# Second feed-forward matmul of a transformer block by seven half-size products over two hidden blocks

## The reference

```python
D_MODEL = 1024; SEQ = 1024; D_FF = 4 * D_MODEL; PLE_DIM = 256
x = x + jnp.concatenate([y_lru, y_att], axis=-1) @ w_out[i]
h = rmsnorm(x, g_ffn[i])
x = x + jnp.square(jax.nn.relu(h @ w_ff1[i])) @ w_ff2[i]
gate = jax.nn.sigmoid(rmsnorm(x, g_ple[i]) @ w_ple_gate[i])
x = x + gate * (p[i] @ w_ple_proj[i])
return rmsnorm(x, g_final)
```

## Time and profile before

| | |
|---|---|
| median of 3 runs | 1074.56 us (1074.12 to 1074.68) |
| profiled execution, first to last instruction | 1072.1 us (its whole time isn't given apart; the median of the runs is 2.5 us above this span) |
| TensorE busy | 1063.0 us, 99% |
| VectorE, ScalarE, GpSimd busy | 680.3, 468.1, 416.6 us |
| passes of the second matmul | 1536, 199.8 + 199.2 + 199.2 us of overlapping durations |
| loads of hidden weights in the loop | 60 of 512 KB, landing 3.8 us after issue |

### The profile page before, as it was taken

The page is one execution under the profiler, slowest core; times in us unless marked ns, Lnnn a source line. Parts: engine busy times, 40 slices in busy tenths (PEclk is TensorE's granted clock), DMA queues, the critical chain, the costliest instruction groups (busy, mean ns, idle before and its releaser), DMA issues.

```text
span 1072.1 us, 13889 instructions
## 1 busy us (share of the span) xinstructions
PE 1063.0 (99%) x4960; PEld 869.5 (81%) x4960; DVE 680.3 (63%) x932; ACT 468.1 (44%) x806; POOL 416.6 (39%) x282
## 2 busy tenths in 40 slices
PE   9999999999999999999999999999999999999997
PEld 7877787777887888888888888888888888888897
DVE  7988787888799643644544544544544544697648
ACT  7467836555683332332332322322322422566334
POOL 0000061334136626516426425435435445295221
PEclk9999999999999999999999999999999999999999
DMA  8111110111011121121111111112112112420004
GB/s 335 40 40 40 40 58 32 40 41 40 0 40 40 40 79 39 39 78 39 39 70 48 39 49 69 39 39 78 39 39 78 39 39 76 159 79 1 1 2 158
DMA packets 20179, 61.06 MB, mean 57 GB/s; under 512 B 2096, under 2 KB 4144, under 8 KB 20144
## 3 DMA queue, kind: packets, MB, share of 16 engines
q1 hardware_dynamic: 19312, 59.56, 15.3%
q10 hardware_dynamic: 832, 1.05, 0.3%
HBM read 56.40 MB, written 4.19 MB: 57 GB/s over the span
## 4 chain that ended last, share of the span: by engine, by line
PE 89%; DVE 6%; ACT 3%; issue 1%; DMA 1%; SPq 0%; POOL 0%; DVEq 0%; ACTq 0%; POOLq 0%
PE bank L611 29%; PE bank L612 28%; PE bank L613 28%; PE bank L726 1%; PE bank L697 1%; ACT raw L1191 1%; DMA stage<-in_w_in 1%; DVE xT L1849 1%; DVE t_lo L1798 1%; PE bank L741 0%; PE bank L756 0%; DVE raw L1792 0%; ACT h_hi L1183 0%; DVE r_ffn L1433 0%; DVE r_mix L1433 0%
## 5 line engine op out<-in xcount | busy, mean ns | idle before, releaser
L611 PE MATMUL bank<-h_hi,w_hi 128*128 128x512 f32 (+1 forms) x722 | 278.5, 386 | 0.6 <-DVE w_lo L1428 0.5
L612 PE MATMUL bank<-h_lo,w_hi 128*128 128x512 f32 (+1 forms) x722 | 274.6, 380 | 0.0
L613 PE MATMUL bank<-h_hi,w_lo 128*128 128x512 f32 (+1 forms) x722 | 274.5, 380 | 0.0
L1849 DVE TENSOR_TENSOR xT<-bank,xT 128x512 f32<-128x512 f32 x256 | 172.3, 688 | 109.8 <-PE bank L613 109.8
L611 PE MATMUL bank<-u_hi,w_hi 128*128 128x512 f32 x512 | 199.8, 390 | 0.2
L613 PE MATMUL bank<-u_hi,w_lo 128*128 128x512 f32 x512 | 199.2, 389 | 0.0
L612 PE MATMUL bank<-u_lo,w_hi 128*128 128x512 f32 x512 | 199.2, 389 | 0.0
L611 PEld LDWEIGHTS bank<-h_hi,w_hi 128*128 128x128 f32 x722 | 135.7, 188 | 35.1 <-issue 6.6
L613 PEld LDWEIGHTS bank<-h_hi,w_lo 128*128 128x128 f32 x722 | 135.8, 188 | 26.1
L612 PEld LDWEIGHTS bank<-h_lo,w_hi 128*128 128x128 f32 x722 | 135.8, 188 | 25.4 <-issue 0.5
L557 POOL TENSOR_TENSOR w_lo<-w_raw,w_hi 128x1024 fp32r<-128x1024 f32 x30 | 73.9, 2485 | 125.6 <-ACT w_hi L1283 117.8
(11 more groups left out here) (238 smaller groups left out, 1727.9 us busy)
## 6 DMA issues: line engine op xcount, KB each, us to landing
w_raw<-in_w_ff SPq DMA_DIRECT2D x60, 512.0 KB, 3.8
stage<-in_w_in SPq DMA_DIRECT2D x13, 512.0 KB, 6.6
stage<-in_w_out SPq DMA_DIRECT2D x8, 512.0 KB, 4.5
stage<-in_w_ple_gate SPq DMA_DIRECT2D x8, 512.0 KB, 3.2
xT<-in_x SPq DMA_DIRECT2D x6, 512.0 KB, 10.9
stage<-in_w_ff SPq DMA_DIRECT2D x4, 512.0 KB, 3.2
out_x<-xT SPq DMA_DIRECT2D x4, 512.0 KB, 3.1
out_x<-xT SPq DMA_DIRECT2D x6, 256.0 KB, 2.2
```

The source lines that it names most:

```text
L611: pe.matmul(o, whi, hh, start=first, stop=False, skip_group_check=onto)
L612: pe.matmul(o, whi, hl, start=False, stop=False, skip_group_check=onto)
L613: return pe.matmul(o, wlo, hh, start=False, stop=last, skip_group_check=onto)
L1849: dve.tensor_tensor(dst, bank[4 + q % 4][:, :], dst, ALU.add).then_inc(y_added, 1)
```

## The change

Blocks 2 to 15 are taken in seven pairs `g`, 1 to 7. In each pair the first matmul is computed as before, 7 products for block s = 0 and 7 for s = 1 (`first_product`, steps t = 0 to 13 of left operands). The second matmul of a pair is also computed by seven products: 4 output tiles x 512 tokens, inner size 2 x 256 over both blocks (`second_product`, p = 0 to 6). The four output tiles are the outer loop; the left operands of the two blocks (t = 14 + 2p + s) the inner one. The sums that Winograd's form needs go over w2's quarters (GpSimd, `w2_sum`), over the hidden values (VectorE, `right_sum`), and over the results: x is kept in a changed basis between pairs (8 additions before pair 1) and folded back in the last pair (`fold`).

All left operands (w1 and w2 alike) now go through a ring of four slots (`LEFTS`), each split for itself: `left_head` on ScalarE, `left_low` on GpSimd. `step_over(t - LEFTS)` makes the split wait until the slot's last user is done. Right operands of the second matmul have four slots too (`right_head` on ScalarE, `right_low` on VectorE). The freed space holds w2 of both blocks unsplit. w1 comes half by half: for s = 1 the first half after left 3 and the second after left 6 are ready. `read_sums` on VectorE adds the four banks of a step p to `xT`, and `second_product` waits for each bank's read (`y_added`) before it writes it again. In the last pair the embedding's splits stand among these instructions (`embedding_high`, `embedding_low`), and the low parts of w_ple_proj have moved from VectorE to GpSimd, ahead of the sums of squares. The gate's rows are taken in the order 4 to 7, 0 to 3.

The diff, cut to its core:

```diff
+PAIRS = FF_BLOCKS // 2
+STEPS = 4 * PRODUCTS
+LEFTS = 4
+RIGHTS = 4
+FF_ORDER = tuple(range(LT, KD)) + tuple(range(LT))
...
+        left_at = (WH + 8 * KB, WH + 12 * KB, ST, ST + 4 * KB)
+        left_hi = [at(f"left_hi{i}", o, [P, LT, P], F32R)[:, :, :] for i, o in enumerate(left_at)]
+        left_lo = [at(f"left_lo{i}", o + 2 * KB, [P, LT, P], F32R)[:, :, :] for i, o in enumerate(left_at)]
+        right_hi = at("right_hi", Y, [P, RIGHTS, HALF], F32R)
+        right_lo = at("right_lo", Y + 8 * KB, [P, RIGHTS, HALF], F32R)
+        u2 = at("u2", Y + 8 * KB + 3 * 2 * KB, [P, HALF])
+        w2_raw = (at("w2_raw0", WH, [P, 2, D]), at("w2_raw1", WL, [P, 2, D]))
...
+        def step_over(eng, g, t):
+            if t < 0 and isinstance(g, int) and g == 1:
+                eng.wait_ge(prod_done, PRODUCTS)
+                return
+            before, t = (1, t + STEPS) if t < 0 else (0, t)
+            if t < 2 * PRODUCTS:
+                eng.wait_ge(prod_done, 2 * PRODUCTS * g + (t - 6 - 2 * PRODUCTS * before))
+            else:
+                eng.wait_ge(ff2_done, STEPS * g + (4 * ((t - 2 * PRODUCTS) // 2) + 8 - STEPS * before))
...
-            with sp.Fori(2, FF_BLOCKS) as b:
-                sp.wait_ge(prod_done, PRODUCTS * b - PRODUCTS)
-                load_w1(b)
-                load_w2(b)
+            with sp.Fori(2, PAIRS) as g:
+                sp.wait_ge(left_ready, counted(10 - STEPS, g))
+                load_w1_half(g, 0, 0)
+                sp.wait_ge(left_ready, counted(17 - STEPS, g))
+                load_w1_half(g, 0, 1)
+                sp.wait_ge(left_ready, counted(27 - STEPS, g))
+                load_w2_pair(g)
+                sp.wait_ge(left_ready, counted(3, g))
+                load_w1_half(g, 1, 0)
+                sp.wait_ge(left_ready, counted(6, g))
+                load_w1_half(g, 1, 1)
...
-            w1_low(2)
-            with pool.Fori(2, FF_BLOCKS - 1) as b:
-                w2_low(b)
-                w1_low(b + 1)
-            w2_low(FF_BLOCKS - 1)
+            def left_low(g, t):
+                pool.wait_ge(left_high, counted(t, g))
+                pool.tensor_tensor(left_lo[t % LEFTS], left_raw(t), left_hi[t % LEFTS], ALU.subtract
+                                   ).then_inc(left_ready, 1)
+            def w1_front(g, s):
+                a11, a21, a12, a22 = (w1_quarter(w_raw, q) for q in range(4))
+                for h in range(2):
+                    pool.wait_ge(w1_half_in[h], 32 * g + 16 * (s - 1))
+                pool.tensor_tensor(a21, a21, a22, ALU.add).then_inc(sum1_made, 1)
+                pool.wait_ge(sum1_made, counted(4 * s, g, 8))
...
+                pool.tensor_tensor(s2_raw(s), a21, a11, ALU.subtract).then_inc(sum1_made, 1)
+            def w1_back(g, s):
+                a21, a12, a22 = (w1_quarter(w_raw, q) for q in (1, 2, 3))
+                pool.wait_ge(sum1_made, counted(4 * s + 1, g, 8))
+                pool.wait_ge(left_ready, counted(PRODUCTS * s + 2, g))
+                pool.tensor_tensor(a21, a22, s2_raw(s), ALU.subtract).then_inc(sum1_made, 1)
+                pool.wait_ge(sum1_made, counted(4 * s + 2, g, 8))
+                pool.tensor_tensor(s2_raw(s), a12, s2_raw(s), ALU.subtract).then_inc(sum1_made, 1)
+            def w2_sum(g, i, s):
...
+                elif i == 2:
+                    pool.wait_ge(left_ready, counted(2 * PRODUCTS - 1, g))
+                    pool.wait_ge(sum2_made, counted(2 + s, g, 8))
+                    ins = pool.tensor_tensor(s4_raw(s), a21, a12, ALU.subtract)
...
+            def left_pair(g):
+                for s in range(2):
+                    w1_front(g, s)
+                    for i in range(3):
+                        left_low(g, PRODUCTS * s + i)
+                    w1_back(g, s)
+                    for i in range(3, PRODUCTS):
+                        left_low(g, PRODUCTS * s + i)
+                        if s == 1 and i in (3, 4):
+                            w2_sum(g, 0, i - 3)
+                for s in range(2):
+                    left_low(g, 14 + s)
+                    w2_sum(g, 1, s)
+                for s in range(2):
+                    w2_sum(g, 2, s)
+                for t in range(16, 20):
+                    left_low(g, t)
+                for s in range(2):
+                    left_low(g, 20 + s)
+                    w2_sum(g, 3, s)
+                for t in range(22, STEPS):
+                    left_low(g, t)
+            left_pair(1)
+            with pool.Fori(2, PAIRS - 1) as g:
+                left_pair(g)
+            left_pair(PAIRS - 1)
+            for h in range(2):
+                o = slice(h * HP, (h + 1) * HP)
+                pool.wait_ge(pw_high, h + 1)
+                pool.tensor_tensor(pw_lo[:, o], pw_raw[:, o], pw_hi[:, o], ALU.subtract).then_inc(pw_ready, 1)
...
-            with pe.Fori(2, FF_BLOCKS) as b:
-                for i in range(PRODUCTS):
-                    if i < 4:
-                        pe.wait_ge((c11_read, u2_made, c12_made, c21_made)[i], b - 1)
-                    product(b, i)
-                pe.wait_ge(w2_split, 2 * b)
-                ff2(b)
+            def first_product(g, t):
+                s, i = t // PRODUCTS, t % PRODUCTS
+                o = bank[(0, 1, 3, 2, 3, 0, 2)[i]][:, :]
+                if i < 4:
+                    pe.wait_ge((c11_read, u2_made, c12_made, c21_made)[i], 2 * g + (s - 1))
+                else:
+                    pe.wait_ge((p5_read, p1_read, c22_made)[i - 4], 2 * g + s)
+                pe.wait_ge(left_ready, counted(t, g))
+                whi, wlo = left_hi[t % LEFTS], left_lo[t % LEFTS]
...
+                last.then_inc(prod_done, 1)
+            def second_product(g, p):
+                onto = p in (1, 3, 5)
+                for m in range(LT):
+                    pe.wait_ge(y_added, read_count(g, p - 1, m))
+                    for s in range(2):
+                        t, j = 2 * PRODUCTS + 2 * p + s, 2 * p + s
+                        if m == 0:
+                            pe.wait_ge(left_ready, counted(t, g))
+                            pe.wait_ge(right_ready, counted(j, g, 2 * PRODUCTS))
+                        last = passes(bank[4 + m][:, :], left_hi[t % LEFTS][:, m, :], left_lo[t % LEFTS][:, m, :],
+                                      right_hi[:, j % RIGHTS, :], right_lo[:, j % RIGHTS, :], s == 0 and not onto,
+                                      s == 1, onto)
+                    last.then_inc(ff2_done, 1)
+            with pe.Fori(1, PAIRS) as g:
+                for t in range(2 * PRODUCTS):
+                    first_product(g, t)
+                for p in range(PRODUCTS):
+                    second_product(g, p)
...
+            def left_head(g, t):
+                step_over(act, g, t - LEFTS)
+                left_raw_in(act, g, t)
+                act.activation(left_hi[t % LEFTS], left_raw(t), ACT.Copy).then_inc(left_high, 1)
+            def right_head(g, j):
+                if j >= RIGHTS:
+                    step_over(act, g, 2 * PRODUCTS + j - RIGHTS)
+                right_raw_in(act, g, j)
+                act.activation(right_hi[:, j % RIGHTS, :], right_raw(j), ACT.Copy).then_inc(right_high, 1)
+            def hidden_square(g, s, i):
+                act.wait_ge(u_scaled, 8 * g + (4 * s + i - 3))
+                u = (relu, usq, late, u21)[i][:, s, :]
+                act.activation(u, u, ACT.Square).then_inc(u_sq, 1)
+            def first_bank(g, s):
...
+            def ff_pair(g, last=False):
+                for t in range(LEFTS):
+                    left_head(g, t)
+                for s in range(2):
+                    t = PRODUCTS * s + LEFTS
+                    first_bank(g, s)
+                    for i in range(4):
+                        left_head(g, t + i)
+                        if s == 1 and i == 0:
+                            right_head(g, 0)
+                    hidden_square(g, s, 0)
+                    left_head(g, t + 4)
+                    hidden_square(g, s, 1)
+                    last_bank(g, s)
+                    if s == 1:
+                        right_head(g, 1)
+                        right_head(g, 2)
+                    left_head(g, t + 5)
+                    hidden_square(g, s, 2)
+                    left_head(g, t + 6)
+                    hidden_square(g, s, 3)
+                right_head(g, 3)
+                for j in range(4, 2 * PRODUCTS):
+                    right_head(g, j)
+                    left_head(g, 14 + j)
+                    if last and j < 10:
+                        embedding_high(j - 4)
...
-            with dve.Fori(1, FF_BLOCKS - 1) as b:
-                hidden(b)
-                for q in range(16):
-                    add_ff(b, q)
+            def post(g, s):
...
+                relu_scale(c12, 0)
+                if s == 1:
+                    right_sum(g, 0, 1)
+                dve.wait_ge(c11_read, 2 * g + s)
+                relu_scale(c11, 1)
+                if s == 1:
```

(63 more changed lines are left out.)

241 lines of the change are left out of this document (190 added, 51 removed).

## The result

The changed kernel takes 1120.83 us (median of 4 runs, 1117.88 to 1121.57) against 1074.59 beside it: ratio 1.0428, 95% interval 1.0413 to 1.0443. It is slower, by 46 us where 18 were forecast, and 0.8 us above the wide range of 1050 to 1120. The profiled execution spans 1119.6 us, 47.5 more than before.

The account below looks back on a forecast made before the run. TensorE, 99% busy, was taken as the bound. Removed matmuls -38.1, pair stalls +48.3, last pair +3 and tail +5 gave +18.2: a span of 1090.3, with a median 2.5 above it, 1092.8 us; range 1080 to 1105, wide 1050 to 1120.

Parts of the forecast that it names:

- the wide range: Whole time of 1050 to 1120 us, leaving out only the rival of no feeding bound and the clock.
- Removed matmuls: Second matmul of each pair: 24 fewer matmuls, 5.44 us a pair, -38.1 us over seven pairs.
- The chain to step 1: GpSimd's late second block, its 19 instructions, then ScalarE and VectorE: TensorE idles 4.6 to 5.7 us, 4.9 taken.
- eleven delays: Within GpSimd's row of 19: 11 VectorE two-operand instructions cost it 0.45 us each, 4.95 us, ending at 42.5.
- Step 3 and steps 4 to 6: Later in each pair's second matmul: TensorE stalls of 1.5 us at step 3, 0.5 together at steps 4 to 6.
- Last pair: VectorE's splits and folds ahead of a read the last step needs: a stall of 0 to 7 us, 3 taken.
- Tail: After the last step, TensorE stalls for later final tiles and GpSimd's moved splits: 0 to 10 us, 5 taken.
- Clock: TensorE at 1.2 GHz instead of 2.4 after idle gaps: no term in the sum, only a rival, chance 0.05.
- Rival 1: Whole kernel: feeding is no bound, TensorE stays full; 1044 us, chance 0.13.
- Rival 3: VectorE and GpSimd always alternate, tail at its upper end: 9.1 us a pair, +37.6, 1112 us; chance 0.17.
- Rival 4: TensorE's idle gaps cost its clock: 10 us of low clock a pair adds 35, 1128 us; chance 0.05.
- full price: Each VectorE two-operand instruction costs GpSimd 0.61 us, not 0.45: 1.8 us more a pair, 12 in all; not adopted.

Follow-up runs that it names:

- experiment 3: Changed kernel with VectorE's later sums over the hidden values placed behind or between the bank reads: 1089.36 us (1.0138).
- experiment 4: Changed kernel with GpSimd's first two sums of w2 ahead of the second block's w1 sums: 1091.37 us (1.0165).
- experiment 1: Changed kernel with VectorE reading a PSUM bank as second operand in most right-operand splits and hidden-value sums, values no longer the reference's: 1076.57 us (1.0021).
- experiment 6: As experiment 5, with the last pair's folds on VectorE behind the reads of step 5's banks: 1080.82 us (1.0061).
- experiment 10: As experiment 9, with two orders of the tail changed, ScalarE's keeps of projections and GpSimd's rest of the sum of squares: 1059.49 us (0.9860).
- experiment 5: Changed kernel with the orders of experiment 3 and experiment 4 together, and ScalarE's right operand 3 ahead of left operand 17: 1081.95 us (1.0076).
- experiment 9: As experiment 6, with high parts of right operands 4 to 13 copied to idle banks for VectorE's splits, and two further VectorE orders: 1059.09 us (0.9859).
- experiment 2: Changed kernel with 17 extra matmuls into an unread bank ahead of step 1 of each pair: 1112.77 us (1.0359).
- experiment 7: Changed kernel with 17 extra matmuls ahead of step 1 and 8 ahead of step 3 of each pair, into an unread bank: 1105.45 us (1.0296).
- experiment 11: As experiment 9 without the copies, keeping only its two further VectorE orders: 1076.90 us (1.0028).

## Why the prediction was right and wrong

- **Removed matmuls**: right, 168 fewer, -38.1.
- **The chain to step 1**: right at every station, within 0.2 us up to right 3's split. The eleven delays it counted in GpSimd's row are there: 11 of the 19 instructions last 1.54 to 1.75 us, the others 1.28 to 1.30. Where the prediction chose ("I take 4.9, since left 18 may only just arrive") the other end came: left 18 is there, step 1 starts at 49.25, and the 1.1 at step 0 and 4.5 at step 1 make 5.6. Experiments 3, 4 and 1 cut the chain in three places and moved step 1 to +46.9, +46.8 and +46.6, all within 0.4 of what the chain says.
- **Step 3 and steps 4 to 6**: 2.05 for 1.5, the engines alternate; 0 for 0.5. A pair's idle time is 7.6 us in place of 6.9, +4.9 in all.
- **Last pair**: +6.9 idle in place of 3, the upper end: the four folds cost not 0.6 each but 2.0 on average, since the row runs into GpSimd's 1024-column splits, where one takes up to 2.87.
- **Tail**: +2.5 in place of 5. Experiments 6 and 10 show that its waits stand in a row behind each other: taking one away brings the next. So 2.5 is not the tail's own cost; it goes with the stall of the last pair: with it experiment 5 has a tail of 126.5 us, without it experiment 6 has 132.1 and 9 has 132.4, against 123.7 before.
- **Clock**: this is the step that failed. The sum had no term for it, and as a rival ("TensorE's idle gaps cost its clock", with the argument "the gaps are 5 us after 40 busy ones") it had 0.05. It cost 20.6 us, more than the forecast's whole loss of 18.2. Experiments 2 and 7 show the cause: with the gaps filled by matmuls that do nothing useful the kernel is 8 and 15.4 us faster, though nothing in the chain is earlier. The argument against it rested on no row: before, no gap of that length stood in a full TensorE of the loop.

The one row that the rival leaned on, an average of 0.95 beside 6.5 us of idle time, was read too coarsely. TensorE's last instruction ends at 1066.6, and cut just behind it the stretch reads:

```profile
1020.00:1066.80 46.80, 45.53 (x328) 42.59 (x326) 33.21 (x59) 22.27 (x41) 11.14 (x10) 1.00 0.18 63
1066.80:1072.10 5.30, 0.00 (x0) 0.00 (x0) 1.84 (x6) 0.17 (x1) 0.73 (x1) 0.50 0.74 247
```

The clock was full as long as TensorE had work and fell when it had none left. The row says that the clock falls with idleness; it says nothing of a loss, since no matmul ran at the low level.

Check of the sum: 18.2 + 4.9 + 3.9 - 2.5 + 20.6 + 2.2 = 47.3, measured 47.5. Without the clock the same count gives +26.7, which would be 1101.3, in the forecast's own range of 1080 to 1105.

Rival 1, that feeding is no bound, comes near in the loop once the contention is away and the orders are mended: pairs of 77.3 us for 76.2. But the kernel then takes 1059, not 1044, for the last pair (84.0) and the tail. Rival 3 (the engines always alternate) was right about the engines; it priced a pair's gaps at 9.1 where 7.6 came, and had no clock in it, so that its 1112 comes within 9 us of the measured time is luck. Rival 4 was right in kind: it took 10 us of low clock a pair, and 6.8 came on average. The rule of the Trainium skill that the prediction cited ("SBUF — State Buffer", "Who interferes with whom") was borne out in kind by experiments 1, 9 and 11: one SBUF operand less, and the median of VectorE's splits of `relu` falls from 1.73 to 0.69 (experiment 1). By its full price, an estimate, the w2 sums would have ended 1.8 us later than the 42.5 that 0.45 gives; they ended at 42.65.

## What to carry to other kernels

When a change adds element-wise work on VectorE and GpSimd together, lay out the chain with contended durations instead of adding up shares, and ask which of VectorE's instructions could read a bank in place of SBUF: copies in idle banks, made by an engine with room, were worth 18 us here, though only once the orders had been mended. Where TensorE is the bound, price new gaps of the size seen here (2 us and more) twice, once for their length and once for a stretch at half speed, 1.7 us or 3.4, and forecast a range that reaches from none of these stretches to one at every gap.
